# Slot tables turned by transposes and decode rows collected by DMA, in the expert stage of a four-layer hybrid step

## The reference

```python
def hier_moe(u, w_rg, b_rg, w_re, b_re, w1, w3, w2):
    ...
    pg_top, g_idx = lax.top_k(pg, 1)
    le = ((x @ w_re).astype(F32) + b_re.astype(F32)).reshape(-1, MOE_GROUPS, MOE_EPG)
    le_g = jnp.einsum('tge,tg->te', le, jax.nn.one_hot(g_idx[:, 0], MOE_GROUPS, dtype=F32))
    top_l, e_idx = lax.top_k(le_g, MOE_TOPK)
    wts = pg_top * jax.nn.softmax(top_l, axis=-1)
    ...
    combine = jnp.einsum('tk,tke->te', wts, jax.nn.one_hot(eid, MOE_EXPERTS, dtype=F32))
    h = jax.nn.silu(jnp.einsum('td,edf->tef', x, w1)) * jnp.einsum('td,edf->tef', x, w3)
    y = jnp.einsum('tef,efd->td', h * combine[:, :, None].astype(h.dtype), w2)
```

## Time and profile before

| | |
|---|---|
| median of 3 runs | 1970.73 us (1969.31 to 1974.62) |
| span of the profiled execution, first to last instruction | 1964.8 us |
| what lies around the span, median less span | 5.9 us |
| TensorE busy, share of the span | 1897.6 us, 97% |
| mean granted TensorE clock | 0.983 |
| VectorE / ScalarE / GpSimd busy | 811.9 / 645.3 / 119.4 us |
| DMA: moved, mean rate | 629.74 MB, 321 GB/s |

### The profile page before, as it was taken

How to read it: one execution, slowest core, us unless ns; L and a number is a source line. 1 busy time by engine, 2 the same in 40 slices (tenths; PEclk the granted TensorE clock), 3 DMA queues, 4 the chain that set the end, 5 groups by cost and what they waited for, 6 DMA issues and landing times. The chain is left out here.

```text
span 1964.8 us, 28506 instructions
## 1 busy us (share of the span) xinstructions
PE 1897.6 (97%) x11091; PEld 1188.8 (61%) x11091; DVE 811.9 (41%) x1908; ACT 645.3 (33%) x1508; POOL 119.4 (6%) x100
## 2 busy tenths in 40 slices
PE   9999999999999887899999999999999999999999
PEld 7877764444777564644445887644437877764443
DVE  4699242232203359242332363323315699242232
ACT  3489121212112217222122425221213489122111
POOL 0233000000100000000000000000000233000000
PEclk9999999999999879999999999999999999999999
DMA  9888949999837986579999468599997788959997
GB/s 333 258 298 257 368 193 420 421 421 403 284 98 264 302 278 292 216 324 421 420 421 340 138 225 329 228 422 420 421 410 238 243 295 265 369 197 421 421 420 327
DMA packets 243172, 629.74 MB, mean 321 GB/s; under 512 B 14184, under 2 KB 169112, under 8 KB 193352
## 3 DMA queue, kind: packets, MB, share of 16 engines
q1 hardware_dynamic: 231176, 613.88, 82.9%
q0 software_dynamic: 2368, 8.48, 1.4%
q10 hardware_dynamic: 9472, 5.28, 0.9%
HBM read 600.39 MB, written 35.56 MB: 324 GB/s over the span
## 5 line engine op out<-in xcount | busy, mean ns | idle before, releaser
L753 PE MATMUL bank<-uT,ring 128*128 128x264 f32 x1280 | 301.1, 394 | 2.4 <-DVE s_xbc L1088 2.4
L1767 PE MATMUL bank<-late,e_room 128*64 128x512 f32 x1280 | 281.1, 593 | 0.6 <-DMA late<-in_moe_w 0.6
L753 PEld LDWEIGHTS bank<-uT,ring 128*128 128x128 f32 x1280 | 245.2, 194 | 51.2 <-issue 7.0
L1767 PEld LDWEIGHTS bank<-late,e_room 128*64 128x64 f32 x1280 | 90.6, 137 | 180.9 <-issue 178.6
L1608 DVE TENSOR_TENSOR e_room<-e_room,bank 128x512 f32<-128x512 f32 x32 | 22.0, 688 | 367.5 <-PE bank L1767 367.5
L1767 PE MATMUL bank<-ring,e_room 128*64 128x512 f32 x768 | 169.7, 594 | 0.0
L1813 PE MATMUL bank<-late,e_room 128*64 128x512 f32 x640 | 143.1, 595 | 6.5 <-DMA late<-in_moe_w 3.8
L1614 DVE TENSOR_TENSOR xT<-xT,bank 128x512 f32<-128x512 f32 x112 | 69.5, 682 | 142.3 <-PE bank L1841 142.3
L1944 ACT ACTIVATE e_room<-bank 128x512 f32<-128x512 f32 x32 | 19.1, 598 | 319.5 <-PE bank L1767 319.4
L850 PE MATMUL bank<-s_xbc,ring 128*128 128x264 f32 x512 | 116.4, 388 | 3.8 <-ACT s_xbc L995 3.8
L1767 PEld LDWEIGHTS bank<-ring,e_room 128*64 128x64 f32 x768 | 53.7, 137 | 106.0 <-issue 105.5
(11 more groups left out here) (548 smaller groups left out, 2477.5 us busy)
## 6 DMA issues: line engine op xcount, KB each, us to landing
late<-in_moe_w SPq DMA_DIRECT2D x240, 1024.0 KB, 19.1
ring<-in_moe_w SPq DMA_DIRECT2D x144, 1024.0 KB, 15.7
ring<-in_m_w_in SPq DMA_DIRECT2D x40, 1024.0 KB, 9.1
late<-in_ssm SPq DMA_DIRECT2D x32, 512.0 KB, 6.7
out_ssm_s<-late SPq DMA_DIRECT2D x32, 512.0 KB, 4.0
ring<-in_m_w_out SPq DMA_DIRECT2D x16, 1024.0 KB, 9.3
late<-in_cache_cmp SPq DMA_DIRECT2D x64, 256.0 KB, 4.8
ring<-in_h_w_in SPq DMA_DIRECT2D x16, 1024.0 KB, 5.8
```

Of the source, the lines that this page charges most:

```text
L753: mm = nc.tensor.matmul(bank[p % 3][:, 0:T], W.view(s, KT, 256)[:, k, c:c + 128], uT[:, k], start=(k == 0), stop=(k == KT - 1))
L1767: mm = nc.tensor.matmul(bank[b][CAP * j:CAP * j + CAP, :], xg[:, EK // 2 * h + k, CAP * j:CAP * j + CAP], rows_of(p, key)[:, k], start=(h ...
```

## The change

The two tables of the prompt tiles are no longer turned by products with `turner`. DVE multiplies the pair's `to_row` by a new value per token and pair, `bound` (`face`): the token's weight, at least 1e-30, where the token has chosen one of the pair's experts, and one less where it only fills a free slot. TensorE transposes the result (two transposes in place of the products of L1783). DVE then makes `turns` by comparing the transposed table with 0 and `slot_weight` by its maximum along the row. ACT's copy into `turns` goes.

The decode tokens are no longer collected by products after each pair. ACT issues two DMAs behind its last copy of a pair, from the first 8 slots of each expert in `yg_dec` to 8 rows of `collect` (128 rows of 1024, one row for each expert and decode token). The next pair's Silu waits for them (`dec_sent`). In the last pair, eight products of `collect` with `dec_w`, the turned weighted table of all experts' decode slots, give the sum over all experts, and one addition puts it into `xT`. `to_first` is weighted once a layer for this and transposed in pair 0. `x_dec` moves to `u_nat[:, 0]`, since `collect` takes its place.

```diff
-        turner, dec_to, dec_sum = sb("turner", [128, 128 + 2 * PAIRS]), sb("dec_to", [128, PAIRS, 32]), sb("dec_sum", [128, D // 4])
+        facing, dec_w = sb("facing", [128, 2, 2, CAP]), sb("dec_w", [128, NB])
...
+        collect = in_room(4232, [NE * NB, D])
+        x_dec = u_nat[:, 0].rearrange("p k (e r) -> p k e r", e=NE)
+        turns, slot_weight = in_room(0, [PAIR, 2, 128]), in_room(256, [PAIR, 2])
...
+                    a = 0 if p == PAIRS - 1 else 1
+                    nc.vector.tensor_tensor(to_row[:, p % 2, a:TT].rearrange("p t e r -> p t (e r)"),
...
+                def face(p):
+
+                    dve.wait_ge(*to_row_ready.now())
+                    nc.vector.tensor_tensor(facing[:].rearrange("p t e r -> p t (e r)"), to_row[:, p % 2, 1:TT].rearrange("p t e r -> p t (e r)"),
+                                            bound[:, :, bass.ds(p, 1)].to_broadcast([128, 2, PAIR]), ALU.mult).then_inc(*to_row_ready.one())
...
-                    link(nc.vector.tensor_copy(turner[:, 0:128], ident))
-                    link(nc.vector.tensor_copy(turner[:, 128:128 + PAIRS], weight[:, 1]))
-                    link(nc.vector.tensor_copy(turner[:, 128 + PAIRS:], weight[:, 2]))
-                    link(nc.vector.memset(dec_to[:], 0.0))
...
+                    link(nc.vector.tensor_scalar(jump[:], jump[:], -1.0, None, ALU.add))
+                    link(nc.vector.scalar_tensor_tensor(out=bound[:], in0=weight[:, 1:TT], scalar=LEAST, in1=jump[:], op0=ALU.max, op1=ALU.add))
+                    link(TTn(to_first[:], to_first[:], comb[:, 0].rearrange("p (e o) -> p e o", o=1).to_broadcast([128, NE, NB]), ALU.mult))
...
+                        dve.wait_ge(*weights_turned.of(p, 1, 1))
+                        if p == 0:
+                            nc.vector.tensor_copy(dec_w[:], bank[SPARE][:, 384 - NB:384]).then_inc(*dec_turned.one())
+                        facing_slots = bank[SPARE][:, 0:2 * 128].rearrange("p (t i) -> p t i", t=2)
+                        nc.vector.tensor_scalar(turns[:], facing_slots, 0.0, None, ALU.not_equal).then_inc(*from_row_ready.one())
+                        nc.vector.tensor_reduce(slot_weight[:], facing_slots, AX.X, ALU.max).then_inc(*from_row_ready.one())
+                        if p + 1 < PAIRS - 1:
+                            face(p + 1)
...
-                            nc.vector.tensor_tensor(dec_sum[:], dec_sum[:], made, ALU.add).then_inc(*dec_added.one())
...
+                    face(0)
+                    nc.vector.memset(collect[:], 0.0).then_inc(*dec_kept.one())
...
-                        for t in (1, 2):
-                            nc.tensor.matmul(bank[SPARE][:, BACK * (t - 1):BACK * t], to_row[:, p % 2, t].rearrange("p e r -> p (e r)"), turner[:],
-                                             start=True, stop=True)
...
+                        for t in range(2):
+                            mm = nc.tensor.transpose(bank[SPARE][:, 128 * t:128 * t + 128], facing[:, t].rearrange("p e r -> p (e r)"), ident)
...
+                        pe.wait_ge(*dec_turned.at(1))
+                        pe.wait_ge(*dec_sent.at(2 * (PAIRS - 1)))
+                        for c in range(KT):
+                            mm = nc.tensor.matmul(bank[X[0]][:, NB * c:NB * c + NB], collect[:, 128 * c:128 * c + 128], dec_w[:], start=True, stop=True)
...
-                        for g in range(4):
-                            mm = nc.tensor.matmul(bank[Y[0]][32 * g:32 * g + 32, 0:D // 4], back_dec, yg_dec[:, D // 4 * g:D // 4 * g + D // 4],
-                                                  start=True, stop=True)
...
                     act.sem_inc(*free_of(p, ("moe_w1", 1, 1)))
+                    if p:
+                        act.wait_ge(*dec_sent.at(2 * p))
                     nc.scalar.activation(sg[:], bank[GATE][:], ACT.Silu).then_inc(*gate_ready.one())
...
-                        nc.scalar.activation(turns[:], bank[SPARE][:, 0:320], ACT.Copy).then_inc(*from_row_ready.one())
...
+                    act.wait_ge(*yg_ready.now())
+                    act.wait_ge(*dec_kept.at(3))
+                    for j in range(2):
+                        e = p + PAIRS * j
+                        act.dma_start(collect[NB * e:NB * e + NB], yg_dec[CAP * j:CAP * j + NB]).then_inc(*dec_sent.one())
```

More of the change, by code:

```diff
@@ L1344, in moe, with weight_in @@
         yg = in_room(3208, [PAIR, D])
-        x_dec = in_room(4232, [128, EK, NE, NB])
-        turns, yg_dec, yg_far = in_room(0, [PAIR, 320]), in_room(1672, [PAIR, D]), in_room(5256, [PAIR, D])
-        BACK = 128 + 2 * PAIRS
+        collect = in_room(4232, [NE * NB, D])
+        x_dec = u_nat[:, 0].rearrange("p k (e r) -> p k e r", e=NE)
+        turns, slot_weight = in_room(0, [PAIR, 2, 128]), in_room(256, [PAIR, 2])
+        yg_dec, yg_far = in_room(1672, [PAIR, D]), in_room(5256, [PAIR, D])
         def back_to(t):
[L1350 to L1357, removed]
+            return turns[:, t - 1]
+        def weight_in(t):
+            return slot_weight[:, t - 1:t]
         GATE, UP, HT, SPARE, Y, X = 0, 1, 2, 3, (4, 5), (6, 7)
@@ L1615, in pair @@
                                                     ALU.add).then_inc(*x_added.one())
[L1616 to L1620, removed]
-                            dve.wait_ge(*dec_added.at(p))
-                            nc.vector.tensor_tensor(dec_sum[:], dec_sum[:], made, ALU.add).then_inc(*dec_added.one())
-                def add_last():
-                    dve.wait_ge(*dec_made.at(PAIRS))
-                    last_tokens = xT[:, :, LP:T].rearrange("p (g h) b -> p h g b", h=2)
-                    for h in range(2):
-                        ins = nc.vector.tensor_tensor(last_tokens[:, h], last_tokens[:, h], bank[X[0]][:, 32 * h:32 * h + 32].rearrange("p (g b) -> p g b", g=4), ALU.add)
-                    ins.then_inc(*dec_added.one())
-                    dve.wait_ge(*dec_added.at(PAIRS))
+                def add_last():
+                    dve.wait_ge(*dec_made.at(1))
+                    nc.vector.tensor_tensor(xT[:, :, LP:T], xT[:, :, LP:T], bank[X[0]][:, 0:KT * NB].rearrange("p (c b) -> p c b", c=KT), ALU.add) \
+                        .then_inc(*dec_added.one())
+                    dve.wait_ge(*dec_added.at(1))
                     for c in range(KT):
@@ L1958, in pair @@
                         half = slice(512 * c, 512 * c + 512)
-                        act.wait_ge(*from_row_ready.at(p + 1))
-                        nc.scalar.activation(yg[:, half], bank[Y[c]][:], ACT.Copy, scale=weight_in(1, p)).then_inc(*yg_ready.one())
-                        nc.scalar.activation(yg_far[:, half], bank[Y[c]][:], ACT.Copy, scale=weight_in(2, p)).then_inc(*yg_ready.one())
+                        act.wait_ge(*from_row_ready.at(2 * p + 2))
+                        nc.scalar.activation(yg[:, half], bank[Y[c]][:], ACT.Copy, scale=weight_in(1)).then_inc(*yg_ready.one())
+                        nc.scalar.activation(yg_far[:, half], bank[Y[c]][:], ACT.Copy, scale=weight_in(2)).then_inc(*yg_ready.one())
                         nc.scalar.activation(yg_dec[:, half], bank[Y[c]][:], ACT.Copy).then_inc(*yg_ready.one())
+                    act.wait_ge(*yg_ready.now())
[3 more added lines that the diff above has]
+                        act.dma_start(collect[NB * e:NB * e + NB], yg_dec[CAP * j:CAP * j + NB]).then_inc(*dec_sent.one())
                 def gathered_program():
```

42 lines of the change are left out of this document (17 added, 25 removed).

## The result

The changed kernel takes 2015.03 us (median of 4 runs, 2006.80 to 2018.05) against 1970.62 us: ratio 1.0200, 95% interval 1.0178 to 1.0221. It is some 40 us slower (44 us between the two medians, 39 us by the ratio); 1977.1 us were predicted, with an upper end of 1985. The profiled execution has a span of 2016.3 us at a mean granted clock of 0.971 (before 1964.8 us, 0.983). The two spans lie 51.5 us apart, more than the medians. In every other run the time is some 1.8 us over the span of the same execution, so the one profiled before took an estimated 1966.6 us, less than its three measured times, while the one profiled after took 2018.05 us, the most of its four. The 5.9 us given above as lying around the span before are therefore 1.8 us, and the rest is scatter.

The account below looks back on a forecast made before the run. The DMA weight stream was taken to bound the expert stages, so PE's savings counted nothing; 1.6 us a layer for the collection, 6.4 us in all, on 1970.7 us gave 1977.1 us, range 1968 to 1985 us.

Parts of the forecast that it names:

- What bounds the stage: Expert stages: the DMA weight stream sets the end, by 1.1 us a layer over PE; PE's savings are waited away.
- PE is the bound: Rival, expert stages: loads wait for slots that PE now frees sooner; 22 to 29 us gained, 1942 to 1949 us; chance 0.07.
- The collection: DMA engines in the expert stages: 14 added transfers lengthen the weight stream by 1.6 us a layer, 6.4 us in all.
- The upper bound: Collection on the DMA engines: at most 3.07 us a layer, if the same eight engines carry every transfer.
- Eight engines carrying a transfer: Rival, collection: the eight engines are those that end last; 2.18 to 3.07 us a layer, 1979.4 to 1983.0 us; chance 0.20.
- the prediction's own signs: DMA step wrong if the last landing stays or moves over 3 us; right if engines stay at 421 GB/s.
- The eight products: PE, last pair: eight products instead of two add 0.85 to 2.5 us, within PE's net gain, which was put at nothing.
- The clock: Rival, pairs 6 and 7: PE's clock falls in new gaps; 3.65 us a layer, about 1992 us; chance 0.04.
- The Silu: ACT, next pair: its wait for collected rows is hidden, 10.8 us available; rival, late landing, about 2018 us, chance 0.04.
- DVE's new work: VectorE, each pair: comparison, maximum and product of about 0.41 us each fit in idle time and cost nothing.

Follow-up runs that it names:

- e1: The changed kernel without its 14 collection transfers a layer, ScalarE raising their semaphore itself; decode tokens' expert output missing: 1982.41 us, 1.0043 to before.
- e11: The kernel before with only the transposed tables, decode rows by products as before, and PE's branch hint behind the routing's twelve transposes: 1973.64 us, 0.9995.
- e9: The changed kernel with the collected rows written to DRAM and not brought back; decode tokens' expert output missing: 1986.89 us, 1.0052 to before.
- e13: The changed kernel with the eight rows of a transfer landing 4 partitions apart instead of next to each other: 1994.56 us, 1.0104 to before.
- e8: The changed kernel without the collection, plus 128 empty instructions in the part of layer 1's program that is not run: 1982.97 us, 1.0045 to before.
- e14: The changed kernel with rows landing 4 partitions apart and PE's branch hint, with its alignment, behind the routing's twelve transposes: 1993.43 us, 1.0098 to before.
- e10: The changed kernel without the collection, PE's branch hint and alignment moved from the routing's head to just ahead of the decode gather: 1998.28 us, 1.0113 to before.

## Why the prediction was wrong

**What bounds the stage: right.** The stream ends it. PE's waits for `late<-in_moe_w` are 7.5 us a layer ahead of the gate and up products (7 or 8 were forecast), but part of that is the slower stream: in e1 they are 5.3 us. PE saves 1.06 us a pair (1.17 predicted; a transpose takes 0.18 us, not 0.11), and e1 and e11 show it worth nothing that can be measured. The rival "PE is the bound" is out.

**The collection: the step that failed**, by its size. It was priced by its bytes, 1.6 us a layer and 3.07 at most. It costs 6.0 us: besides the bytes, which e9 confirms (7.8 packets against 8), weight packets take longer while rows land in a few partitions. The upper bound counted the time of the engines that carry the rows, and not what their landing does to the weight packets beside them. Eight engines carrying a transfer, as weighed, did not set the price: e9 and e13 move the same eight rows a transfer and lose 7.8 and 16.1 packets. By the prediction's own signs the step was wrong too: the stream went from 421 to 410 GB/s, and the last landing moved by more than 3 us.

**The eight products: hidden only where the clock holds.** They last 1.69 us, inside the 0.85 to 2.5 us more that were predicted. From the last landing to the stage's end it is 3.79 us in all four layers before, the time of the last 16 down products. After, it is 3.80 and 4.11 us in layers 1 and 2: there the end stands where the last load would put it or just behind, and the products cost 0.3 us at most. In layers 0 and 3 it is 5.44 and 4.78 us, and there a stretch at 1.2 GHz falls on the down products. e1 has the same: 4.04 and 3.87 us in layers 1 and 2, 5.67 and 6.08 us in layers 0 and 3, where its down products ran at 1.2 GHz. On average stage less stream grew from 7.4 to 8.2 us. The cover was used up, so that the lower clock came through.

**The clock: partly.** The last layer's chain has 8.64 us for its 32 down products where pair 1 has 7.02 us; the records show 1.2 GHz there from 2000.4 to 2003.8 us, behind PE's waits. All four stages after have such a stretch, none before; in layers 1 and 2 it does not fall on the last down products. It costs 1.6 us of this chain, not the 3.65 us priced, and no more than 0.8 us a stage in the mean.

**The Silu: right.** The last row has landed 4.7 us (median; at most 5.5) after issue, and the Silu is still released by PE; that rival is out. DVE's new work ends no wait of the transposes back.

**Outside the stages: a term that was missing.** The prediction had no term for the rest of the layers and so put it at nothing, without a reason. Of the 24.3 us between the profiles, 7.0 fall in layer 0, 10.9 in layer 1, 3.2 in layer 2 and 3.1 in layer 3. e1 and e8, whose stages are no longer than before, are 0.43% and 0.45% slower in 9 and 10 runs, so some 8 us of the outside go with the new decode path, even without its transfers; e11, the tables alone, has none of it. Layer 2 has the wait at the alignment's branch (3.2 us more than before); layer 0 has one too in this execution (4.03 us against 1.04), as in some other profiles but not all. In layer 1's mixer 75 us were granted at 1.2 GHz, 51 before. This last part stays open: that mixer takes 356 to 364 us in the profiles without the new decode path and 360 to 369 us in those with it, and one profile a kernel can't part it from scatter.

## What to carry to other kernels

Where a saturated stream ends a stage, price a small transfer beside it by where it lands, not by its bytes alone: rows in neighbouring partitions cost five times their bytes here, rows four partitions apart twice, rows in DRAM once. And take work off PE only where PE ends the stage; an engine at 97% of the span was not the bound in any of these four stages.

## What the runs showed of the hardware that was not expected

Two transfers of 32 KB inside SBUF brought what the core's DMA engines moved from 421 to about 320 GB/s for 3 us, while their own packets were not slow (162 ns for 4 KB). With the same bytes the loss beyond the rows' own depended on where they landed: 35.9 packets a pair in neighbouring partitions, 8.1 four partitions apart, none in DRAM. The branch that the alignment of the code leaves took 3.6 us in one layer of e1 and 3.7 us in one of e14, and 0.3 to 0.4 us in the others, and a hint that ran 2.8 us ahead of its branch left a wait of 3.17 us behind it (e10).
